# Gates of a hybrid decoder block as seven block products, their weight sums made once on GpSimd, and the router weights scaled earlier

## The chip, the cores and the metric

The kernel runs on one core of a Trainium2 chip, as one program with one launch. The metric is the device time of that core in microseconds. Three runs of the kernel before gave 1765.0, 1762.42 and 1762.63 us, median 1762.63. All arithmetic is in float32, and every float32 matmul of the program stands in the trace as two instructions.

## The reference, cut to what matters

The reference is a decoder block over 2048 tokens of 1024 channels: a normalised input goes through one wide projection, whose parts feed four mLSTM heads and a gated convolution; an output projection, a second norm, a router and 32 experts follow.

```python
hn = rms_norm(x, norm_mix)
proj = hn @ w_in + b_in                       # 1024 -> 4*512 + 2*4 + 3*512
q, k, v, o, ig, fg, cb, cc, cx = split(proj)  # o: 512 wide, ig and fg: 4 each
h_m = mlstm_chunkwise(q / sqrt(128), k, v, ig, log_sigmoid(fg))
y_m = sigmoid(o) * h_m
y_c = cb * causal_conv3(cc * cx)
x   = x + concatenate([y_m, y_c]) @ w_out
hn2 = rms_norm(x, norm_ffn)
x   = x + hier_moe(hn2, ...)                  # top-1 of 4 groups, top-2 of its 8 experts
return rms_norm(x, norm_final)
```

The change is about `o`, `ig` and `fg` (the output, input and forget gates: 520 columns of the wide projection), about the weights of the router inside `hier_moe`, and about one transpose in the expert part.

## The kernel before, in words

The tokens go through the mixer in four blocks (b = 0 to 3) of 512, 245 us each; then come the experts, from 937 us to the end. Inside a block TensorE works in this order: the q and k columns, the gates (`o` and the eight gate columns), the v columns, the convolution columns, which are woven among the mLSTM chunks (four chunks of 128 tokens), and the output projection, among whose products stand the router's logits (`router_logits`, L869) of the same block.

Nearly all of these products are block products in seven parts. A 2 x 2 split of both operands gives four block results from seven products of block sums (in place of eight products of plain blocks). `rounds` (L746) does it for q, k and the convolution, `v_part` (L808) for v, `out_part` (L775) for the output projection. The sums of weights for v and for the output projection are made once, in block 0, by GpSimd (`w_v_sums`, L1637, and `w_out_sums`, L1593), and stored to memory; later they are loaded like any weights. `weight_sums` (L1584 to L1591) makes those of the rounds anew for each slot of columns. The sums of tokens (`xsum`) are made once for each block by VectorE and serve all of them.

The gates are the exception. `tokens_out` (L779 to L789) computes them plainly: for each half s of the columns (256, and 264 with the eight gate columns in the second half) and each of four tiles of 128 tokens, eight matmuls over the 1024 input channels, into two banks of PSUM by turns; VectorE (L2368, L2370) reads each tile with its bias added and so frees its bank. In block 0 alone the gates are computed at the very start by another function.

Each engine runs its instructions in the order of the code. SyncE's queue (SP) loads the weights into two buffers `ww`, each load behind a wait for the work that frees its half; ScalarE's queue (ACT) moves keys, attention rows and `x2` rows; GpSimd's queue (POOL) has the sums, the indirect transfers and a few plain ones. At the end of a block POOL does, in this order: the `over_cleared` copy (L1708), `weight_sums(b + 1, 0)` for the first round of the next block, `norm_scales(b + 1)` (L1551, L1554), and then for each of the four tiles of the block the scale `rs2` of the second norm (L1724, L1732). For that scale ScalarE first squares the tile (`squares_of`, L1360) into the buffers `hn2`; VectorE then multiplies by it (L2274). SP brings the tile back turned by quarters into `attn` (`load_x2_quad`, L519), VectorE transposes it there (L2284), and TensorE computes the router's logits from it.

The router's weights `wrt` are multiplied once by the second norm's channel weights: eight VectorE instructions at the end of block 0 (L2575 to L2579), ahead of the reads of the output projection (`out_reads`).

In the expert part, the lists of items are built by VectorE (L2859 to L2876) while the first items already run: `hidden(1)` (L2734) and `x_turned(2)` (L2740) of item 1 and item 2 stand among the list's instructions, and TensorE's products of the next item (L1156) wait for the second.

## Time and profile before

| | |
|---|---|
| runs | 1765.0, 1762.42, 1762.63 us (median 1762.63) |
| profiled execution | 1765.43 us |
| its span, first to last instruction | 1763.7 us |
| mean granted clock of TensorE | 0.998 |
| TensorE busy | 1744.4 us, 99% of the span |
| VectorE, ScalarE, GpSimd busy | 942.2, 236.5 and 678.9 us |
| moved from and to memory | 370.78 and 68.72 MB |

The profiled execution lies 2.8 us above the median and 0.43 us above the first of the three runs. The span leaves out 1.7 us that lie around it. "Busy" counts overlapping instructions once; an engine that waits for another is not busy, and its row in a list of waits names the instruction that came last.

### The profile page before, as it was taken

The page shows a single profiled execution, that of the slowest core. Times are in us where ns is not written, and L with a number is a line of the kernel's source. Part 1 is how long each engine was busy: PE and PEld are TensorE (multiplying, and loading weights), DVE is VectorE, ACT ScalarE, POOL GpSimd, SP SyncE. Part 2 cuts the span into 40 slices and gives each one's busy share as a digit, 9 for nine tenths or more (in the row PEclk, how much of TensorE's full clock was granted, in tenths as well). Part 3 has the DMA queues.
Part 4 walks back from the last instruction along what each step waited for, and adds up shares of the span by engine and source line. Part 5 has one row for each costly group of instructions (what it writes and reads, how often), then busy time and mean ns, then how long its engine had stood idle before and what let it go on. Part 6 is the DMA issues. An engine that isn't in the chain of part 4 may idle for free. (4 is left out here: it accounts for less than half of the span.)

```text
span 1763.7 us, 27714 instructions
## 1 busy us (share of the span) xinstructions
PE 1744.4 (99%) x10013; PEld 1393.6 (79%) x10013; DVE 942.2 (53%) x1913; ACT 236.5 (13%) x618; POOL 678.9 (38%) x755
## 2 busy tenths in 40 slices
PE   9999999999999999999999999999999999999997
PEld 8889658888478887588895678887777778887776
DVE  5666785378773687763785783333423233323332
ACT  2021110211101211102210201101111101101011
POOL 4943212044221235130341125445455455554552
PEclk9999999999999999999999999999999999999999
DMA  7663742344632437423444489998988999998984
GB/s 289 229 242 109 274 168 91 123 146 170 248 117 99 144 114 272 154 95 126 155 135 140 164 329 345 349 343 326 343 349 331 339 352 338 347 341 331 349 328 174
DMA packets 135755, 415.31 MB, mean 235 GB/s; under 512 B 54838, under 2 KB 69486, under 8 KB 102320
## 3 DMA queue, kind: packets, MB, share of 16 engines
q1 hardware_dynamic: 57488, 316.78, 48.4%
q0 software_dynamic: 26880, 58.91, 9.4%
q10 hardware_dynamic: 51248, 37.82, 6.6%
q8 instruction: 81, 1.33, 0.3%
q14 instruction: 58, 0.48, 0.1%
HBM read 370.78 MB, written 68.72 MB: 249 GB/s over the span
## 5 line engine op out<-in xcount | busy, mean ns | idle before, releaser
L1134 PE MATMUL ps_proj<-hnT,wo 128*128 128x128 f32 (+4 forms) x992 | 199.5, 283 | 0.0
L1136 PE MATMUL ps_proj<-hnT,wo 128*128 128x128 f32 (+4 forms) x992 | 197.6, 281 | 0.0
L1134 PEld LDWEIGHTS ps_proj<-hnT,wo 128*128 128x128 f32 x992 | 153.7, 191 | 13.6 <-issue 13.6
L1748 POOL DMA_INDIRECT xin<-hn_rows,idx_quad x116 | 117.4, 1012 | 116.2 <-DVE hnT L2748 44.0
L1136 PEld LDWEIGHTS ps_proj<-hnT,wo 128*128 128x128 f32 x992 | 153.0, 191 | 0.0
L746 PE MATMUL ps_proj<-hnT,ww 128*128 128x256 f32 x640 | 151.9, 379 | 0.0
L746 PEld LDWEIGHTS ps_proj<-hnT,ww 128*128 128x128 f32 x640 | 119.8, 190 | 16.6 <-issue 1.4
L1584 POOL TENSOR_TENSOR xres<-ww 128x512 f32<-128x512 f32 x12 | 15.3, 1271 | 291.0 <-DMA ww<-in_w_slots 279.6
L2972 DVE SCALAR_TENSOR_TENSOR hn<-xin,rsy,ww 128x1024 f32<-128x1024 f32 x30 | 38.5, 1284 | 134.9 <-POOL rsy L1806 134.9
L1136 PE MATMUL ps_rows<-hnT,wo 128*128 128x128 f32 (+4 forms) x496 | 98.8, 281 | 0.0
L1134 PE MATMUL ps_scores<-hnT,wo 128*128 128x128 f32 (+4 forms) x496 | 98.8, 281 | 0.0
L1136 PE MATMUL ps_scores<-hnT,wo 128*128 128x128 f32 (+4 forms) x496 | 98.8, 281 | 0.0
L1134 PE MATMUL ps_rows<-hnT,wo 128*128 128x128 f32 (+4 forms) x496 | 98.8, 281 | 0.0
L775 PE MATMUL ps_proj<-wo,yT 128*128 128x512 f32 x192 | 88.8, 599 | 0.0
L787 PE MATMUL ps_proj<-ww,hnT 128*128 128x256 f32 (+1 forms) x384 | 84.7, 382 | 0.0
L2734 DVE TENSOR_TENSOR kT<-qT,ps_proj 128x128 f32<-128x128 f32 (+4 forms) x62 | 15.6, 294 | 127.4 <-ACT qT L1440 127.2
L787 PEld LDWEIGHTS ps_proj<-ww,hnT 128*128 128x128 f32 x384 | 73.0, 190 | 11.2
L1134 PEld LDWEIGHTS ps_scores<-hnT,wo 128*128 128x128 f32 x496 | 76.5, 191 | 0.0
L1136 PEld LDWEIGHTS ps_scores<-hnT,wo 128*128 128x128 f32 x496 | 76.5, 191 | 0.0
L1136 PEld LDWEIGHTS ps_rows<-hnT,wo 128*128 128x128 f32 x496 | 76.5, 191 | 0.0
L1134 PEld LDWEIGHTS ps_rows<-hnT,wo 128*128 128x128 f32 x496 | 76.5, 191 | 0.0
L746 PE MATMUL ps_proj<-xin,ww 128*128 128x256 f32 x320 | 76.4, 380 | 0.0
(522 smaller groups left out, 3494.5 us busy)
## 6 DMA issues: line engine op xcount, KB each, us to landing
wo<-in_w_gu SPq DMA_DIRECT2D x128, 1024.0 KB, 7.6
ww<-in_w_slots SPq DMA_DIRECT2D x43, 1024.0 KB, 4.9
og<-in_w_dn SPq DMA_DIRECT2D x32, 1024.0 KB
vx<-in_w_dn SPq DMA_DIRECT2D x32, 1024.0 KB
xin<-in_x SPq DMA_DIRECT2D x16, 512.0 KB, 5.8
ww<-w_v_sums SPq DMA_DIRECT2D x16, 512.0 KB, 3.9
xres<-in_x SPq DMA_DIRECT2D x16, 512.0 KB, 5.4
x_rows<-x ACTq DMA_DIRECT2D x16, 512.0 KB, 3.4
```

Of the source, the lines that this page charges most:

```text
L746: mm = pe.matmul(place, w_(k), x_[:, k, :], start=(new and k == 0), stop=(k == KH - 1), skip_group_check=True)
L775: mm = pe.matmul(place, y_[:, k, :], w_[:, k, :], start=(new and k == 0), stop=(k == KH - 1), skip_group_check=True)
L787: mm = pe.matmul(PROJ[:, n % 2, 0:w], hnT[:, k, t * P:(t + 1) * P], slot_weights(slot, k, 0, w), start=(k == 0), stop=(k == KT - 1))
L1134: pe.matmul(GU[m][:, 0:n_], wo[:, kt, m * P:(m + 1) * P], xT[:, kt, 0:n_], start=(kt == 0), stop=(kt == KT - 1), skip_group_check=True)
L1136: mm = pe.matmul(GU[m][:, CAP:CAP + n_], wo[:, kt, FF + m * P:FF + (m + 1) * P], xT[:, kt, 0:n_], start=False, stop=(kt == KT - 1), skip_g ...
L1584: pool.tensor_tensor(wsum(s, 1, first), a21, a22, ALU.add).then_inc(ready, 1)
L1748: pool.indirect_dma_start(xg[:, t * TC:(t + 1) * TC], None, hn2_d.rearrange("s (j c) -> (s j) c", j=TQ), bass.IndirectOffsetOnAxis(ap=idx_ ...
L2734: i_ = dve.tensor_tensor(hT[:, m, 0:n_], sgt[:, m, 0:n_], src[:, CAP:CAP + n_], ALU.mult)
L2972: dve.scalar_tensor_tensor(out=fo, in0=yr[:], scalar=rsy[:, 1, 0:1], in1=gfin, op0=ALU.mult, op1=ALU.mult).then_inc(S_("out_rows_ready"), 1)
```

## The change

It has four parts.

1. In blocks 1 to 3 `o_part` (L842 after) computes the gates as seven products of eight matmuls with 260 columns each: a weight slot now holds 256 columns of `o` and four gate columns in each half. The seven products go into four pairs of banks (`NUM`, `SR`, `STA`, `PROJ`), eight VectorE instructions (`o_reads`) put the results together, and SP loads their weights half a slot at a time (`load_o`).
2. The four sums of gate weights are made in block 0 by GpSimd and stored as `wg_d` (`load_w_gates`, `w_gate_sums`). The columns are cut in two: the first 128 columns of every input block with the four gate columns (j = 0), and the other 128 (j = 1). The buffers are `attn`, the tail slots and `hn2`; the instructions stand on GpSimd between the `over_cleared` copy of block 0 and the scales of the second norm. ScalarE's `squares_of` of tiles 0 and 1 and SP's `load_x2_quad` wait for the last store (`SUMS_STORED`).
3. The eight scalings of `wrt` move from the end of block 0 to its v products: three ahead of the first read of v, five behind it.
4. `x_turned(2)` moves ahead of seven small instructions of the item list, right behind `hidden(1)`.

```diff
-    WG = WC + 2 * H
+    WG = WC + H
-            def tokens_out(b, kind, s, t, slot, first):
-                n = number[(kind, (s, t))]
...
-                w = WG if slot == OG else WC
-                for k in range(KT):
-                    mm = pe.matmul(PROJ[:, n % 2, 0:w], hnT[:, k, t * P:(t + 1) * P], slot_weights(slot, k, 0, w),
-                                   start=(k == 0), stop=(k == KT - 1))
+            def o_part(b, i):
+                s, n = o_loaded(b, i)
+                pe.wait_ge(s, n)
...
+                if i in (2, 3, 4):
+                    pe.wait_ge(S_("o_read"), o_read(b, {2: "p1", 3: "u2", 4: "c22"}[i]))
+                x_ = {1: hnT[:, 0:KH, 0:TH], 2: hnT[:, KH:KT, 0:TH], 3: hnT[:, KH:KT, TH:TB],
+                      4: xsum[3], 5: xsum[0], 6: xsum[1], 7: xsum[2]}[i]
+                w_ = o_place(i).rearrange("p (k c) -> p k c", c=WG)
+                for m in range(2):
+                    for k in range(KH):
+                        mm = pe.matmul(O_BANK[i][:, m, 0:WG], x_[:, k, m * P:(m + 1) * P], w_[:, k, :],
+                                       start=(i not in (2, 4) and k == 0), stop=(k == KH - 1), skip_group_check=True)
+                mm.then_inc(S_("o_part_done"), 1)
...
-                for s in range(2 if b > 0 else 0):
-                    for t in range(CT):
-                        tokens_out(b, "o", s, t, 4 + s, t == 0)
+                for i, buf, half in (V_PARTS if b > 0 else ()):
+                    o_part(b, i)
...
                 def squares_of(t):
+                    if t < 2:
+                        act.wait_ge(S_("w_v_sums_stored"), SUMS_STORED)
...
+            def load_w_gates(j):
+                if j == 0:
+                    pool.wait_ge(S_("update_done"), CT)
+                else:
+                    pool.wait_ge(S_("part_done"), part_end(0, NS - 1, 4))
+                for n in range(4):
+                    for at, tiles in gate_sums_views(j):
+                        src = w_slots[4 + n // 2, :, (n % 2) * OQ:(n % 2 + 1) * OQ].rearrange("p (k c) -> p k c", c=WG)
+                        pool.dma_start(tiles[n], src[:, :, at]).then_inc(S_("w_v_loaded"), 16)
+            def w_gate_sums(j):
...
+                pool.wait_ge(S_("w_v_loaded"), 64 + (128 if j == 0 else 192))
+                for step, (to, first, op, second) in enumerate(((3, 2, ALU.add, 3), (2, 0, ALU.subtract, 2),
+                                                                (0, 3, ALU.subtract, 0), (1, 1, ALU.subtract, 0))):
+                    for at, tiles in views:
+                        i_ = pool.tensor_tensor(tiles[to], tiles[first], tiles[second], op)
+                    i_.then_inc(made, 1)
+                    pool.wait_ge(made, 4 + j * 4 + step + 1)
+                for n, a in enumerate((3, 0, 2, 1)):
+                    for at, tiles in views:
+                        dst = wg_d[n].rearrange("p (k c) -> p k c", c=WG)[:, :, at]
+                        pool.dma_start(dst, tiles[a]).then_inc(S_("w_v_sums_stored"), 16)
...
+                with pool.If(b < 1):
+                    load_w_gates(0)
+                    w_gate_sums(0)
+                    load_w_gates(1)
                 with pool.If(b < NB - 1):
                     weight_sums(b + 1, 0)
...
                 with pool.If(b < NB - 1):
                     norm_scales(b + 1)
+                with pool.If(b < 1):
+                    w_gate_sums(1)
...
+                router_weights(range(3))
                 v_reads(("p1",))
+                router_weights(range(3, KT))
...
-                dve.wait_ge(S_("consts_loaded"), 16 * NCONST)
-                if b < 1:
-                    for k in range(KT):
-                        i_ = dve.tensor_scalar(wrt[:, k, :], wrt[:, k, :], gffn_c[:, k:k + 1], None, ALU.mult)
-                    i_.then_inc(S_("router_consts"), 1)
...
                     if n_ == NE:
                         hidden(1)
+                        x_turned(2)
...
-                    if n_ == NE:
-                        x_turned(2)
```

On GpSimd at the end of block 0 the kernel before has, from the `over_cleared` copy to the first scale of the second norm (`og` holds the sums of the next block's first round, `ssx` and `st` the scales):

```order
L1708 DMA hn_rows<-in_x 16x16384
L1584 TENSOR_TENSOR og<-ww 128x512 [waits yn_ready]
L1587 TENSOR_TENSOR og<-og,ww 128x512 [waits wsum_ready]
L1588 TENSOR_TENSOR og<-ww 128x512
L1591 TENSOR_TENSOR og<-ww,og 128x512 [waits wsum_ready]
L1551 TENSOR_SCALAR ssx<-ssx 128x4 [waits ss_ready]
L1554 TENSOR_TENSOR ssx<-ssx,mhalf 128x4 [waits ms_ready]
L1724 TENSOR_SCALAR st<-st 128x1 [waits ss2_ready]
L1732 TENSOR_TENSOR st<-st,mhalf 128x1 [waits hn2_ready,ms2_ready]
```

The changed kernel has at the same place (one of each repeated pair of loads, sums and stores is shown, the last column of a DMA is its pieces):

```order
L1802 DMA hn_rows<-in_x 16x16384
L1731 DMA attn<-in_w_slots 128x4x128 [waits update_done]
L1731 DMA slots_tail<-in_w_slots 128x4x4
L1741 TENSOR_TENSOR attn<-attn 128x512 [waits w_v_loaded]
L1747 DMA w_gate_sums<-attn 512x1x128 [waits w_v_sums_made]
L1747 DMA w_gate_sums<-slots_tail 512x1x4
L1731 DMA hn<-in_w_slots 128x4x128 [waits part_done]
L1642 TENSOR_TENSOR og<-ww 128x512 [waits yn_ready]
L1609 TENSOR_SCALAR ssx<-ssx 128x4 [waits ss_ready]
L1741 TENSOR_TENSOR hn<-hn 128x512 [waits w_v_loaded]
L1747 DMA w_gate_sums<-hn 512x1x128 [waits w_v_sums_made]
L1824 TENSOR_SCALAR st<-st 128x1 [waits ss2_ready]
```

Between the copy and the first scale now stand 12 loads, 12 instructions of sums and 12 stores; the sums of the next block's first round are behind 20 of these DMAs, and the first scale of the second norm is behind all of them.

On TensorE the gates of a later block stand in the kernel before, between the k columns (L746) and the v columns, as eight tiles, of which these are the first, the second, the third and the fifth:

```order
L787 MATMUL ps_proj<-ww,hnT 128x256 [waits sums_out,w_loaded0]
L787 MATMUL ps_proj<-ww,hnT 128x256 x7
L787 MATMUL ps_proj<-ww,hnT 128x256 [waits sums_out]
L787 MATMUL ps_proj<-ww,hnT 128x256 [waits bank_emptied]
L787 MATMUL ps_proj<-ww,hnT 128x264 [waits bank_emptied,w_loaded1]
```

In the changed kernel they are these products, each with seven more matmuls behind the one that carries the waits:

```order
L842 MATMUL ps_num<-ww,hnT 128x260 [waits yn_ready,w_loaded0]
L842 MATMUL ps_scores_rows<-ww,xin 128x260 [waits out_read,slots_ready,second_loaded0]
L842 MATMUL ps_state<-ww,xin 128x260 [waits logits_emptied,out_read,w_loaded1]
L842 MATMUL ps_num<-ww,hnT 128x260 [waits o_read,second_loaded1]
L842 MATMUL ps_proj<-ww,xin 128x260 [waits sums_out,w_loaded0]
L842 MATMUL ps_state<-ww,hnT 128x260 [waits o_read,w_loaded1]
L842 MATMUL ps_scores_rows<-ww,xin 128x260 [waits o_read,second_loaded1]
```

Eight tiles became seven products of the same number of matmuls, over six banks more, and each product now waits for its own half slot of weights.

## Rows read from the trace of the kernel before

**Rows 1.** The page, part 1: busy us, share of the span, instructions.

```profile
PE 1744.4 (99%) x10013; PEld 1393.6 (79%) x10013; DVE 942.2 (53%) x1913; ACT 236.5 (13%) x618; POOL 678.9 (38%) x755
```

**Rows 2.** Timeline, TensorE and VectorE, block 1 (start, us, engine, line, form).

```profile
304.49 28.22 PE L787 MATMUL ps_proj<-ww,hnT 128*128 128x256 f32 x128
332.54 3.62 PE L808 MATMUL ps_proj<-ww,hnT 128*128 128x256 f32 x16
...
305.95 0.17 DVE L2167 SCALAR_TENSOR_TENSOR slot_i<-rank,expert 128x8 int32<-128x8 f32 x1
```

**Rows 3.** DMA issues of the whole span: size each, median us to landing.

```profile
ww<-in_w_slots SPq DMA_DIRECT2D x14, 512.0 KB, 4.1
```

**Rows 4.** Timeline, VectorE and TensorE, block 0's end and v columns.

```profile
200.75 4.48 DVE L2578 TENSOR_SCALAR wrt<-wrt,by_channel 128x64 f32<-128x64 f32 x8
206.99 0.69 DVE L2465 TENSOR_TENSOR uu<-uu,yT 128x512 f32<-128x512 f32 x1
...
207.78 3.67 PE L775 MATMUL ps_proj<-kT,uu 128*128 128x512 f32 x8 [2.20 <-issue]
...
86.06 4.82 DVE L2362 TENSOR_TENSOR bvd<-bias 128x256 f32<-128x256 f32 x1
90.91 0.69 DVE L2343 TENSOR_TENSOR vx<-ps_proj,bias 128x512 f32<-128x512 f32 x1
...
96.30 1.89 PE L808 MATMUL ps_proj<-ww,hnT 128*128 128x256 f32 x8
```

**Rows 5.** Timeline, VectorE and TensorE, the item lists of the expert part.

```profile
1051.33 0.28 DVE L2734 TENSOR_TENSOR kT<-qT,ps_rows 128x128 f32<-128x128 f32 x1
...
1055.34 0.63 DVE L2740 STREAM_TRANSPOSE hnT<-xin 128x256 f32<-128x256 f32 x1 [0.18 <-DVE idx_out L2874]
...
1056.03 1.98 PE L1156 MATMUL ps_num<-og,kT 128*128 128x512 f32 x4 [1.05 <-DVE hnT L2740]
```

**Rows 6.** Timeline, TensorE, GpSimd and VectorE, the end of block 0.

```profile
185.57 1.06 PE L992 MATMUL ps_state<-vx,attn 128*128 128x129 f32 x8
...
201.16 1.28 POOL L1584 TENSOR_TENSOR og<-ww 128x512 f32<-128x512 f32 x1 [18.28 <-DMA ww<-in_w_slots]
...
209.75 1.37 POOL L1554 TENSOR_TENSOR ssx<-ssx,mhalf 128x4 f32<-128x4 f32 x1
...
228.01 0.19 POOL L1724 TENSOR_SCALAR st<-st 128x1 f32<-128x1 f32 x1 [2.60 <-ACT hn L1360]
...
220.56 0.87 DVE L1963 TENSOR_SCALAR zz<-ident,ssx 128x128 f32<-128x128 f32 x4
```

**Rows 7.** GpSimd's groups of DMA issues: busy us, mean ns, idle before.

```profile
L1748 POOL DMA_INDIRECT xin<-hn_rows,idx_quad x116 | 117.4, 1012 | 116.2 <-DVE hnT L2748 44.0 <-DVE hnT L2740 42.9 <-issue 26.5
...
L1603 POOL DMA_DIRECT2D w_out_sums<-x x2 | 1.1, 556 | 0.0
...
L1671 POOL DMA_DIRECT2D slots<-slots_main x1 | 0.5, 521 | 0.0
```

**Rows 8.** DMA issues: of 187 to 199 us, then a store of the whole span.

```profile
ww<-in_w_slots SPq DMA_DIRECT2D x1, 1024.0 KB, 13.6
...
w_v_sums<-xres POOLq DMA_DIRECT2D x2, 512.0 KB, 4.0
```

**Rows 9.** Timeline, ScalarE, SyncE's queue, VectorE, TensorE: block 0's first tiles.

```profile
226.67 1.06 ACT L1360 ACTIVATE hn<-x 128x1024 f32<-128x1024 f32 x1 [2.28 <-DVE x L2632]
...
225.94 7.11 SPq L519 DMA_DIRECT2D attn<-x_rows  x8
...
228.88 1.29 DVE L2274 SCALAR_TENSOR_TENSOR hn<-x,st,late 128x1024 f32<-128x1024 f32 x1 [1.77 <-POOL st L1732]
...
233.36 2.10 DVE L2284 STREAM_TRANSPOSE hn2T<-attn 128x512 f32<-128x512 f32 x2
...
236.27 1.09 PE L869 MATMUL ps_state<-hn2T,wrt 128*64 128x128 f32 x16
```

**Rows 10.** Timeline, TensorE at the start of the span.

```profile
1.24 4.87 PE L849 MATMUL ps_rows<-ones 128*128 128x128 f32 x24 [1.24 <-POOL ones L1495]
```

More of the change, by code:

```diff
@@ L152, in build @@
         x2 = [x2_pair[:, i, :] for i in range(2)]
-        hn2 = [sb(f"hn2_{i}", [P, D]) for i in range(2)]
+        hn2_pair = sb("hn2", [P, 2, D])
+        hn2 = [hn2_pair[:, i, :] for i in range(2)]
         rows = [buf[0:H, j * TB:(j + 1) * TB] for buf in (*x2, *hn2) for j in range(2)]
@@ L593, in _ @@
+                for used, i in ((1, 5), (6, 3), (2, 4)):
+                    sp.wait_ge(S_("v_part_done"), v_part_end(b, used))
+                    own_instruction(sp)
+                    load_v(b, i)
+                for n in range(8, SLOTS_B):
                     slot_free(sp, b, n - 2)
@@ L1279, in _ @@
                     own_instruction(act)
-                exp_o(0)
-                exp_o(1)
+                for n, (s, t) in enumerate(EXP_ORDER):
+                    if n % 2 == 0:
+                        act.wait_ge(S_("o_read"), o_read(b, ("c11", "c22", "d12", "c21")[n // 2]))
+                    half = og4[:, t, s, 0:WC]
+                    act.activation(half, half, ACT.Exp, scale=-1.0).then_inc(S_("exp_o_ready"), 1)
+                    act.wait_ge(S_("exp_o_ready"), 2 * (b * 2 * CT + n) + 1)
+                    own_instruction(act)
+                    act.activation(half, half, ACT.Copy, bias=1.0).then_inc(S_("exp_o_ready"), 1)
                 with act.If(b < 1):
@@ L3051, in _packed @@
         cols += [conv + dm + s * wc, conv + 2 * dm + s * wc, conv + s * wc]
-    w_slots = np.zeros((len(cols), P, d // P * (wc + h2)), np.float32)
+    hh = h2 // 2
+    w_slots = np.zeros((len(cols), P, d // P * (wc + hh)), np.float32)
     for n, c in enumerate(cols):
-        w = by_partition(w_in[:, c:c + wc + (h2 if c + wc == gates else 0)])
+        more = gates + (n - 4) * hh if n in (4, 5) else 0
+        w = by_partition(np.concatenate([w_in[:, c:c + wc], w_in[:, more:more + (hh if more else 0)]], axis=1))
         w_slots[n, :, :w.shape[1]] = w
```

259 lines of the change are left out of this document (164 added, 95 removed).

## The prediction

> **What bounds the kernel now.** I read the totals of the engines first. TensorE is busy for 1744.4 us, 99% of the span [rows 1], so the time changes only by fewer or shorter TensorE instructions, by an end of one of TensorE's waits, or by a new wait. Then I read TensorE's rows, where the time between two starts is the price, then the rows of the engines that feed it at the four places of the change, and last the prices of GpSimd's DMA issues and the times to their landing.
>
> **The gates (part 1).** In block 1 the gates begin at 304.49 and the v columns at 332.54: 28.05 us for eight tiles, 128 instructions [rows 2]. Half of them have 256 columns and half 264, so 0.2191 us is the price of one with 260, and that is what all of the new ones have. Seven products of 16 instructions take 112 x 0.2191 = 24.5 us, 3.5 less. With three blocks that is **-10.5 us**.
>
> Does anything eat it? The products need half slots of 512 KB, which land 4.1 us after their issue [rows 3], and SP can issue each of them some 7 us, two products, ahead. The v columns of the kernel before are loaded half by half as well, and the row of TensorE's that begins with the first of them shows no wait [rows 2]. The second product also waits for the routing slots of the block before, which VectorE makes at 305.95 [rows 2]; it would start at 308.0. So I take nothing. The reads take a bank pair each: a VectorE read of 512 columns of PSUM costs 0.69 [rows 4], eight of them 5.6 of 24.5 us. The weight sums for the gates are 260 wide in place of 256, nothing beside it. In block 0 the first gates have 260 columns in both halves (64 instructions of 256 and 64 of 264 before): no difference.
>
> **The router's weights (part 3).** Before, eight scalings hold VectorE from 200.75 for 4.48 us; the sums of tokens behind them end at 207.68, and TensorE's next product starts at 207.78 after 2.20 us of waiting [rows 4]. Without the scalings that wait ends (4.48 earlier is more than 2.20), at this place **-2.2 us**. It counts only if nothing later in block 0 waits anyway, see below. At their new place, 86 to 96 us, VectorE is at the biases for 4.82 us and reads the first v product at 90.91, and TensorE's third v product needs that read at 96.30 [rows 4]. Ahead of the read now come a second such instruction and three scalings (0.56 each at the old price, 1.7). If the second one isn't held, 0.7 like the read, they fit into the 5.4 us that are free, with 0.69 for the read; if it takes 4.82 like the first, TensorE waits 1.8. I take nothing, and 1.8 as the upper end.
>
> **The transpose (part 4).** TensorE waits 1.05 us for the transpose at 1055.34, and `hidden(1)` ends at 1051.6, so it can stand 3.7 us earlier [rows 5]. **-1.0 us**; behind it the hidden products feed on, and the lists of items, 0.6 us later, aren't waited for.
>
> **GpSimd's sums (part 2).** This is what the prediction turns on. The trace has no such DMA, so I follow the queue from the last step of block 0's cell state, 186.6 [rows 6].
> - Eight loads. A POOL issue of 128 rows costs 0.556, of 32 rows 0.521 [rows 7], which is 0.36 ns a row; with 512 pieces I get 0.70. The lower bound is 0.556 (rows cost nothing more), the upper the 1.01 of an indirect issue with the 0.23 of idle time that stands before each (26.5 of "issue" for 116) [rows 7], 1.24. I take 0.70, the nearest. The loads are issued by 192.2. Between 187 and 199 a load of SP took 13.6 us to its landing [rows 8], so the DMA engines are far from idle, and I let the last piece land 6 us after its issue, at 198.2 (the lower end is 194.5, the upper 216 to 221, if the small pieces get through only behind SP's loads).
> - Sums of j = 0: four steps one behind the other, each 1.28 and a small one of 0.19 and a wait of about 0.18 [rows 6], and 1 us for VectorE's instructions that share the port with them: 7.6, until 205.8.
> - Eight stores and four loads, 12 x 0.70 = 8.4 and 0.3: 214.5.
> - The sums of the next block's first round start at 201.16 before and take 5.2 (four of 1.28 and a wait); they end now at 219.7. Then the scales of the next block, 1.7: 221.4. Before, they ended at 211.1, and VectorE first used them at 220.56 [rows 6]; the 0.9 us by which it is late there only hold up work that waits longer further on.
> - Sums of j = 1: 4 x (1.28 + 0.18) = 5.8, and four stores, the last issued at about 229.8; a store of such a size landed 4.0 after its issue [rows 8]. **The last store is there at 233.8.**
>
> Who waits? ScalarE's squares of tiles 0 and 1 and SP's loads into `attn`. The square of tile 1 starts at 226.67 before, and SP's load at 225.94 [rows 9]. The squares come in a row on ScalarE, so that of tile 1 starts 1.7 us after the release, at 235.5: 8.8 later. From there it goes by the order before: the scale on GpSimd at 228.01 [rows 6], VectorE's multiplication at 228.88, the transpose of the tile out of `attn` at 233.36, done 2.10 later, and the router's logits on TensorE at 236.27 [rows 9], with 0.8 us to spare. SP's loads go 7.9 later and come to the same. All else in VectorE's queue behind the multiplication, the output products' reads too, is late by the same. So the logits start **8.0 us** later than before.
>
> That takes the gain of part 3: the earlier 2.2 us of TensorE only make it wait longer at the logits. Its worth is nothing. It waits for some 8 to 10 us there, over four times its wait at 207.78. What follows a rest is seen at the start of the span: 24 filler matmuls of 128 columns take 4.87 us there [rows 10], and eight of 129 columns 1.06 in the middle of the block [rows 6], from start to start about 0.11, so 24 would be 2.8; the start from rest cost 2 us. I take **+2.0** for the clock, which would be at its lower level, 1.2 GHz, for a while after such an idle stretch (bounds 0 and 4).
>
> **Sum**, against the profiled execution's 1765.43 (span 1763.7 and 1.7 around it): -10.5 - 1.0 + 8.0 + 2.0 = -1.5, 1763.9. The profiled execution lies 2.8 above the median of the runs, so I put the new median at 1762.63 - 1.5 = 1761.1 and up, **1762**, within 0.2% (3.5 us) of it, which is what a measurement of this kernel can tell from no change.
>
> **A rule of the Trainium skill.** GpSimd's issue price has the largest lever: of the chain to the last store some 15 issues lie in it, after the loads of j = 0, so 0.1 us more costs 1.5. The Trainium skill, "DMA: Bandwidth & Descriptors", section "Anatomy of one DMA — SWDGE (gpsimd) path", says that many descriptors can be written before their cost shows. By that 512 pieces cost what 128 do, 0.556, and the time is that of A below. In the other direction goes "SBUF — State Buffer", section "SBUF: two separate sides": GpSimd can't write descriptors while VectorE holds the port pair that they share. VectorE's 4.82 us for a sum of 256 columns beside GpSimd's sums [rows 4] agrees with the lock, in the other sense. No run here shows it for descriptors.
>
> **Rivals.**
> - *A, quicker queue.* Each issue costs 0.556 and the loads land at their lower end, 194.5. The stores are then 3.7 + 15 x 0.14 = 5.8 earlier in place, at 228, and the logits are late by 8.0 - 5.8 = 2.2 to 4; with 1 to 2 for the clock: -11.5 + 3 + 1.5 = -7, **1756**. For it: the flat issue prices of 32 and 128 rows [rows 7]. Against: SP's slow load at the same time [rows 8]. It would be fully hidden, at -13.7, **1749**, if the last store landed by 223, for which the chain would have to be 11 us shorter than mine; A's 5.8 is all that the rows give.
> - *B, slower: dear pieces.* If a DMA of 512 pieces is paid like an indirect one, 1.24, the chain grows by 15 x 0.54 = 8.1 us, and all of it reaches the logits: -1.5 + 8.1 = +6.6, **1769 to 1771**. It decides from 0.80 us for one issue (there the sum is nought; at 1.03 it is +3.5). For it: the indirect issues, 116 of one line alone, are the only ones in the trace that cost more than 0.7, and no row shows a direct one of 512 pieces, so the step from 0.556 may be a large one. If besides the small pieces wait behind SP's loads (13.6 us to their landing [rows 8]), the loads of j = 0 land at 216 to 221 and the logits are late by 26 to 31 us: **1782**.
> - *C, the gates don't come cheaper*: 512-KB loads, drains or banks hold TensorE between the products (each would have to lose 0.5 us a product to undo it). For it: 16 waits stand ahead of the seven products; against: the v columns without a wait [rows 2]. With the stall it would be 1772.
> - *D, the clock stays up*: 2 less, **1760**. For it: the 2.20 us of idle time at 207.78, after which the products keep their 3.6 us [rows 4]; against: these are a quarter of what is to come.
>
> **How the numbers follow.** My sum with D, 1759 to 1765: 0.42. A: 0.24 (fully hidden 0.04 of it). B: 0.22 (0.07 of it the second part). C: 0.07. A remainder of 0.05 lies on both sides. The range 1755 to 1776 holds my sum, most of A and the first part of B and C; outside are full hiding and SP's loads ahead, some 0.15 to 0.2. Faster by over 0.2% is below 1759.1: A, and the lower edge of my sum with D, 0.34. Slower is above 1766.2: B, C and a part of the remainder, 0.34. Between them 0.32.
>
> **What would show it.** Right, if the v columns of block 1 start 24.5 us after the gates; if GpSimd's issues with 512 pieces last 0.6 to 0.8 us; if ScalarE's square of tile 0 ends an idle stretch at 234 with the store as its releaser; if the logits of tile 0 follow an idle TensorE of 8 to 10 us near 244; if the waits at 207.78 and 1056.03 are gone. Wrong, if TensorE has no idle time at the end of block 0, or one of over 14 us, or if the gaps between the gates' products exceed those inside them.

## The result, and the profile after

The changed kernel takes 1775.79 us (median of 4 runs, 1773.32 to 1777.41) against 1762.53 of the kernel before on the same chip (4 runs): ratio 1.0064 [1.005, 1.0079], slower by 13 us. Each experiment below is compared in the same way with the kernel before on its own chip, where that kernel's median was 1762.5 to 1764.4. The profiled execution of the changed kernel took 1775.77, with a span of 1774.0; that is 10.3 more than the 1763.7 of before, whose profiled execution lay 2.9 above its median.

TensorE does less, as planned. Part 1 of the page of the changed kernel answers to [rows 1]:

```profile
PE 1738.3 (98%) x9965; PEld 1386.4 (78%) x9965; DVE 945.5 (53%) x1898; ACT 234.7 (13%) x618; POOL 708.9 (40%) x791
```

48 instructions (16 in each of three blocks) and 6.1 us of busy time are gone, and the span has grown by 10.3: 16.4 us are new idle time. The list of TensorE's waits in the changed kernel (source line, releaser, us in total, times, longest) shows where it lies (a releaser "issue" means that the profile shows nothing that the engine waited for):

```profile
PE ps_state L927 <- issue: 11.5, 1, 11.5
PE ps_scores_rows L872 <- DVE zz L2063: 5.2, 1, 5.2
PE ps_state L1216 <- issue: 1.9, 1, 1.9
...
PE ps_scores_rows L1177 <- DVE hnT L2858: 1.2, 1, 1.2
```

The 2.20 at 207.78 [rows 4] and the 1.05 at 1056.03 [rows 5] are gone, and two smaller ones have come up in the experts (1.9 and 1.2, the last two lines). TensorE's timeline in the changed kernel (start, us, engine, line, form, and in brackets the idle time before it with its releaser) shows the end of block 0 and the gates of block 1:

```profile
205.33 3.60 PE L817 MATMUL ps_proj<-kT,uu 128*128 128x512 f32 x8
...
219.06 3.60 PE L817 MATMUL ps_scores_rows<-vx,yT 128*128 128x512 f32 x8
227.91 2.05 PE L872 MATMUL ps_scores_rows<-zz,ones 128*128 128x512 f32 x2 [5.25 <-DVE zz L2063]
229.75 5.44 PE L817 MATMUL ps_proj<-wo,yT 128*128 128x512 f32 x8
...
238.46 3.60 PE L817 MATMUL ps_proj<-kT,cc 128*128 128x512 f32 x8
253.56 1.98 PE L927 MATMUL ps_state<-hn2T,wrt 128*64 128x128 f32 x16 [11.51 <-issue]
...
260.14 3.60 PE L817 MATMUL ps_scores_rows<-qT,cc 128*128 128x512 f32 x8
...
323.57 3.67 PE L842 MATMUL ps_num<-ww,hnT 128*128 128x260 f32 x16
...
348.11 3.62 PE L865 MATMUL ps_proj<-ww,hnT 128*128 128x256 f32 x16
```

The seven gate products go from 323.57 to 348.11 in steps of 3.50 or 3.51 without a gap: 24.54 us for the 28.05 of [rows 2]. The loss lies ahead of them. The norm rows (L872) wait 5.25 us, the router's logits of tile 0 (L927) 11.51, and the logits start at 253.56 instead of 236.27 [rows 9], 17.3 late. What the logits wait for is VectorE's transpose of the tile, which ends at 253.45. The products behind either wait take longer than their 3.60. The windows of the changed kernel (stretch, its length, busy us of PE, PEld, DVE, ACT and POOL with counts, then the granted clock, DMA share, GB/s) say why:

```profile
228.00:230.00 2.00, 2.00 (x3) 0.97 (x4) 1.90 (x4) 0.00 (x0) 0.00 (x0) 0.50 0.93 320
...
253.00:257.00 4.00, 3.44 (x18) 2.44 (x19) 3.66 (x6) 0.28 (x1) 0.00 (x0) 0.50 0.00 0
257.00:263.00 6.00, 6.00 (x16) 2.70 (x15) 5.28 (x7) 0.00 (x0) 0.00 (x0) 0.97 0.00 0
```

Behind each wait the granted clock is 0.50, the level of 1.2 GHz, and 0.97 to 1.00 a few microseconds later. GpSimd's timeline in the changed kernel shows the chain that the logits wait for, at the place of [rows 6]:

```profile
186.84 0.80 POOL L1731 DMA_DIRECT2D attn<-in_w_slots  x1 [4.01 <-PE ps_state L1052]
...
192.07 0.75 POOL L1731 DMA_DIRECT2D slots_tail<-in_w_slots  x1
205.09 1.26 POOL L1741 TENSOR_TENSOR attn<-attn 128x512 f32<-128x512 f32 x1 [12.27 <-DMA slots_tail<-in_w_slots]
...
211.41 0.72 POOL L1747 DMA_DIRECT2D w_gate_sums<-attn  x1 [0.29 <-POOL slots_tail L1741]
...
216.51 3.77 POOL L1731 DMA_DIRECT2D hn<-in_w_slots  x4
219.53 2.04 POOL L1642 TENSOR_TENSOR og<-ww 128x512 f32<-128x512 f32 x1
...
225.81 1.04 POOL L1612 TENSOR_TENSOR ssx<-ssx,mhalf 128x4 f32<-128x4 f32 x1
230.56 5.29 POOL L1741 TENSOR_TENSOR hn<-hn 128x512 f32<-128x512 f32 x4 [3.71 <-DMA hn<-in_w_slots]
236.15 3.00 POOL L1747 DMA_DIRECT2D w_gate_sums<-hn  x4 [0.29 <-POOL hn L1741]
```

In this chain GpSimd stands still twice, for its own loads: 12.27 us for those of j = 0 and 3.71 for those of j = 1. The last store lets ScalarE go at 242.72 (timeline of ScalarE, changed kernel: the square of tile 0; that of tile 1 follows at 243.78, where [rows 9] has 226.67):

```profile
242.72 1.06 ACT L1418 ACTIVATE hn<-x 128x1024 f32<-128x1024 f32 x1 [29.11 <-DMA w_gate_sums<-hn]
```

The DMA issues of two stretches of the changed kernel, 187 to 207 and 206 to 245 us (form, queue, count, KB each, median us to landing), answer to [rows 8]:

```profile
ww<-in_w_slots SPq DMA_DIRECT2D x2, 1024.0 KB, 21.2
attn<-in_w_slots POOLq DMA_DIRECT2D x4, 256.0 KB, 8.7
...
hn<-in_w_slots POOLq DMA_DIRECT2D x4, 256.0 KB, 11.2
```

GpSimd's loads took 9 to 11 us each. SP's two slot loads took 21.2 on the median; the one issued at 187.17, which is that of [rows 8], took 19.3 instead of 13.6. From 190 to 205 the windows show a DMA share of 0.96 to 1.07: the 16 DMA engines were full. In the kernel before they were full as well from 190 to 199 (0.97 to 1.05). Two windows of the changed kernel, columns as above:

```profile
193.00:196.00 3.00, 3.00 (x16) 2.64 (x15) 1.84 (x4) 0.00 (x0) 0.00 (x0) 1.00 1.06 377
221.00:224.00 3.00, 1.66 (x4) 0.38 (x2) 0.00 (x0) 0.00 (x0) 2.82 (x3) 1.00 1.01 121
```

In the second, while the loads of j = 1 are under way, the engines are as full, but they move a third of the bytes (e9 returns to it).

### The profile page after: what moved, and what is told of

It reads as the page before. It is cut to its first block and busy times, and to the rows that moved or that the text cites. A ratio compares the mean times of both kernels' runs of the same rounds, so it can differ in the third digit from the quotient of the medians.

```text
span 1774.0 us, 27704 instructions
## 1 busy us (share of the span) xinstructions
PE 1738.3 (98%) x9965; PEld 1386.4 (78%) x9965; DVE 945.5 (53%) x1898; ACT 234.7 (13%) x618; POOL 708.9 (40%) x791
## 3 DMA queue, kind: packets, MB, share of 16 engines
q0 software_dynamic: 28416, 63.17, 10.3%
## 5 line engine op out<-in xcount | busy, mean ns | idle before, releaser
L1196 PE MATMUL ps_scores_rows<-hnT,wo 128*128 128x128 f32 (+4 forms) x992 | 197.7, 281 | 0.0
L1194 PE MATMUL ps_scores_rows<-hnT,wo 128*128 128x128 f32 (+4 forms) x992 | 197.7, 281 | 0.0
L1194 PEld LDWEIGHTS ps_proj<-hnT,wo 128*128 128x128 f32 x992 | 153.8, 191 | 13.6 <-issue 13.6
L1194 PEld LDWEIGHTS ps_scores_rows<-hnT,wo 128*128 128x128 f32 x992 | 153.0, 191 | 0.0
L1196 PEld LDWEIGHTS ps_scores_rows<-hnT,wo 128*128 128x128 f32 x992 | 153.0, 191 | 0.0
L788 PE MATMUL ps_proj<-xin,yT 128*128 128x256 f32 x312 | 72.3, 381 | 0.4 <-POOL yT L1645 0.4
L3053 DVE SCALAR_TENSOR_TENSOR xin<-ps_state,wgt,xin 128x512 f32<-128x512 f32 x31 | 23.3, 751 | 91.2 <-DMA xin<-x_rows,idx 90.6
L817 PEld LDWEIGHTS ps_proj<-wo,yT 128*128 128x128 f32 x192 | 36.4, 196 | 40.1 <-issue 39.4
L788 PEld LDWEIGHTS ps_proj<-xin,ww 128*128 128x128 f32 x320 | 60.6, 190 | 8.6 <-issue 0.5
L788 PE MATMUL ps_proj<-xin,xres 128*128 128x256 f32 x288 | 66.1, 379 | 0.0
L788 PEld LDWEIGHTS ps_proj<-xin,yT 128*128 128x128 f32 x312 | 58.5, 190 | 8.8 <-issue 1.3
```

Source lines behind the costliest of these rows:

```text
L788: mm = pe.matmul(place, w_(k), x_[:, k, :], start=(new and k == 0), stop=(k == KH - 1), skip_group_check=True)
L817: mm = pe.matmul(place, y_[:, k, :], w_[:, k, :], start=(new and k == 0), stop=(k == KH - 1), skip_group_check=True)
L1194: pe.matmul(GU[m][:, 0:n_], wo[:, kt, m * P:(m + 1) * P], xT[:, kt, 0:n_], start=(kt == 0), stop=(kt == KT - 1), skip_group_check=True)
L1196: mm = pe.matmul(GU[m][:, CAP:CAP + n_], wo[:, kt, FF + m * P:FF + (m + 1) * P], xT[:, kt, 0:n_], start=False, stop=(kt == KT - 1), skip_g ...
L3053: dve.scalar_tensor_tensor(out=h_, in0=y, scalar=wgt[:, col:col + 1], in1=h_, op0=ALU.mult, op1=ALU.add).then_inc(S_("y_emptied"), 1)
```

## The experiments

**e1: the change without the sums.** The seven products read plain halves of the weights, and nothing is loaded, added or stored on GpSimd for them. The gates are then other numbers and so is the routing; only the stages up to the output projection of block 3 compare. Its time, 2311 us, has other work of the experts in it and says nothing here.

```diff
-                with pool.If(b < 1):
-                    load_w_gates(0)
-                    w_gate_sums(0)
-                    load_w_gates(1)
...
-                with pool.If(b < 1):
-                    w_gate_sums(1)
```

> The changed kernel without the sums of gate weights: GpSimd makes none, nobody waits for their stores, and the four products that need sums load plain halves of the gate weights in their place, so the gates of blocks 1 to 3 are other numbers. Theory: all that the change loses is lost at the end of block 0, in TensorE's waits of 5.25 and 11.51 us and the low clock behind each. Then what is left is the gain of the gates (3 x 3.5), of the router's weights (2.2) and of the transpose (1.05), less the 3.1 us of new waits that the changed kernel has in the expert part: 1762.5 - 10.5 - 2.2 - 1.05 + 3.1 = 1752, and 1749 if those waits aren't of the change. No idle time of TensorE above 1 us between 198 and 300 us. Rival: the seven products or their reads and loads cost something too, in blocks 1 to 3; then the time is above 1757 and the gates' stage takes more than 24.6 us.

TensorE's timeline at the start of that projection, in the kernel before, the changed kernel and e1:

```profile
935.87 3.60 PE L775 MATMUL ps_proj<-wo,yT 128*128 128x512 f32 x8
...
945.02 3.60 PE L817 MATMUL ps_proj<-wo,yT 128*128 128x512 f32 x8
...
922.19 3.60 PE L817 MATMUL ps_proj<-wo,yT 128*128 128x512 f32 x8
```

(The experts' products follow from 1004 us in the kernel before, and not from 937, as its description in words has it.) So the seven products and the moved scaling bring 13.7 by themselves, and the sums at the end of block 0 cost 22.8. In e1 TensorE has no wait over 0.5 us between 62 and 989, and the seven products take the same 24.54 us. The loss up to the experts is in this one place; no product, drain or bank takes any (rival C falls).

**e2 and e3: one small part alone, in the kernel before.** e2 moves only the transpose, e3 only the router's scalings.

```diff
                         hidden(1)
+                        x_turned(2)
...
-                    if n_ == NE:
-                        x_turned(2)
```

> The kernel before with the transpose of item 2 right behind the hidden products of item 1, nothing else. Theory 1 (the prediction's): TensorE's wait of 1.05 us near 1056 goes, nothing comes in its place: 1761.5. Theory 2 (from the trace of the changed kernel): with that wait gone, the weights of the next item are loaded a microsecond earlier, while the rows of x gathered for item 0 are still under way; these land some 6 us later, VectorE adds them late, and TensorE waits 1.9 us at the next item: 1763.4, no gain or a small loss.

> The kernel before with the router's weights scaled among the value products, nothing else. Theory: the wait of 2.20 us at 207.78 goes and no other one comes in block 0, since the stall at the logits that ate it in the changed kernel is not there: 1760.3. Rival: some other wait of block 0's end takes its place (the logits stand 0.8 us behind VectorE's transposes): 1762 to 1762.5.

e2: 1763.01 against 1763.57, ratio 0.9988 [0.9979, 0.9997]; the wait of 1.05 is gone and none comes in its place. e3: 1762.3, ratio 0.9992 [0.9983, 1.0001]; the wait of 2.20 is gone and the gates of block 1 start at 301.38 in place of 304.49. In the traces each does what the prediction priced, and both intervals hold that price; e3's also holds no change, so its time alone would not show the gain.

**e4 and e5: the sums at the start of block 0**, from weights that lie in the buffers `ww` for TensorE anyway: ScalarE copies two halves, GpSimd adds into `x2`, `attn` and `slots_tail`, which are free there. e4 stores them through SP's queue, e5 through ScalarE's.

```diff
             load_w_v()
+            gate_sum(0)
+            gate_sum(1)
+            gate_sum(2)
             weight_sums(0, 0)
+            gate_sum(3)
...
+                            for m, a in enumerate((2, 0, 3, 1)):
+                                for c in range(2):
+                                    at = (slice(0, WC), slice(WC, WG))[c]
+                                    sp.dma_start(wg_d[m].rearrange("p (k c) -> p k c", c=WG)[:, :, at], gate_places(a)[c]
```

> The changed kernel with the same sums made elsewhere: at the start of block 0, from the gate weights that lie in the weight buffers for the first gates anyway (no loads). ScalarE copies the first slot's two halves into x2, GpSimd makes three sums from 20 us on and the fourth behind the sums of the first round, SyncE's queue stores them behind the router's weights. Nothing of the gates is left at the end of block 0. Theory: the stall at the end of block 0 was a matter of the place only; here GpSimd is idle from 22 to 29 and from 37 to 41 us, and the four sums take 10.5 us, so nearly nothing waits: 1750 to 1753. Rival 1: the sums push GpSimd's sums of the first round (29.0 us, needed at 37.6) behind, TensorE waits 2 to 6 us near 38: 1753 to 1758. Rival 2: eight stores among the loads of 36 to 52 us hold up the weights of the second slot: a wait near 48, the same price.

> The kernel with the sums at the start of block 0 again, with one difference: the eight stores of the sums go through ScalarE's queue, behind its exponentials (47 us), in place of SyncE's. In the run before this, TensorE waited 10.63 us at 71.65 for the weights of the fourth slot, whose load stood in SyncE's queue behind these stores (issued from 41.4 to 62.1, where the load was issued at 48.15 without them), and 1.32 at 117. Theory: that queue was all of it; without it the time is 1765.8 - 12 = 1754, or below, with no idle time of TensorE over 1 us before 900 us. Rival: the stores' small pieces hold up the DMA engines themselves, whichever queue they come from; then the fourth slot's weights or those of the value products are late by 3 us or more again: above 1757.

e4: 1765.83 against 1763.57, ratio 1.0007 [0.9998, 1.0016]. The waits at the end of block 0 are gone, but there is a new one; the timeline of TensorE and of SP's queue (e4):

```profile
71.65 3.67 PE L809 MATMUL ps_proj<-hnT,ww 128*128 128x256 f32 x8 [10.63 <-DMA ww<-in_w_slots]
...
42.75 7.04 SPq L611 DMA_DIRECT2D w_gate_sums<-x  x1
49.84 4.19 SPq L611 DMA_DIRECT2D w_gate_sums<-slots_tail  x1
...
62.13 1.36 SPq L551 DMA_DIRECT2D ww<-in_w_slots  x2
```

The eight stores hold SP from 41.40 to 62.09, two of them for 7.04 and 4.19 us, and the next weights, issued at 48.15 in the changed kernel, go out at 62.13. My expectation of 1750 to 1753 left that out; my second rival named it, at 2 to 6 us. e5: 1760.22 against 1764.0, ratio 0.9981 [0.9972, 0.999]; I expected 1754. The blocked issues now stand on ScalarE, where they hold up no load of weights, but the stores land late, and GpSimd, which waits for them ahead of the output weights' sums, makes TensorE wait 6.08 us at 81.41. Timelines of ScalarE's queue and of GpSimd (e5):

```profile
49.53 8.25 ACTq L1367 DMA_DIRECT2D w_gate_sums<-slots_tail  x1
...
73.67 4.93 POOL L1698 TENSOR_TENSOR hn<-wo 128x512 f32<-128x512 f32 x4 [8.37 <-DMA w_gate_sums<-slots_tail]
```

**e6: another order on GpSimd at the old place**: all loads first, then every sum, the scales of the next block among them, all stores last.

```diff
                     load_w_gates(0)
-                    w_gate_sums(0)
                     load_w_gates(1)
+                    w_gate_sums(0)
...
                     w_gate_sums(1)
+                    store_gate_sums(0)
+                    store_gate_sums(1)
```

> The changed kernel with the same work on GpSimd at the end of block 0 in another order: both groups of loads first, then the sums of j = 0, the sums of the next block's first round and the scales of its norm, the sums of j = 1, and all twelve stores last. Theory: the first idle stretch (5.25 us, for the scales) goes, since the scales end near 218 and are needed near 219; the second stays in good part, since the stores are still issued one by one and land at 235 to 240, against 242 before: 1760 to 1766. Rival: the DMA engines are the limit and not the order, the loads only land later when they are issued together; then the stall at the logits is as long or longer, and the sum stays at 1772 to 1778.

1773.03 against 1764.0, ratio 1.0049 [1.0034, 1.0064]; I expected 1760 to 1766. Timelines of GpSimd, TensorE and ScalarE (e6):

```profile
204.63 1.26 POOL L1744 TENSOR_TENSOR attn<-attn 128x512 f32<-128x512 f32 x1 [2.49 <-DMA slots_tail<-in_w_slots]
...
234.36 3.60 PE L817 MATMUL ps_proj<-kT,cc 128*128 128x512 f32 x8
251.32 1.98 PE L927 MATMUL ps_state<-hn2T,wrt 128*64 128x128 f32 x16 [13.36 <-issue]
...
240.48 1.06 ACT L1418 ACTIVATE hn<-x 128x1024 f32<-128x1024 f32 x1 [23.16 <-DMA w_gate_sums<-hn]
```

The loads of j = 0 land as late as in the changed kernel. The norm rows no longer wait (they start at 226.64; a wait of 3.62 at 219.67 has come up ahead of them), and TensorE begins its last product ahead of the logits at 234.36, 4.1 earlier than in the changed kernel. Yet the logits start only 2.24 earlier, and that is just what the last store gains (240.48 for 242.72), since the stores now come behind everything. So the logits go by the last store, and the first wait is contained in the second.

**e7 and e11: the clock.** Idle matmuls ahead of the two waits keep TensorE busy, so that the cost of the low clock can be told from that of the wait; they fill the waits and don't shorten them. In e7 there are 23 and 50 matmuls (two instructions each), in e11 23 and 63.

```diff
+            def keep_warm(n):
+                for i in range(n):
+                    pe.matmul(NUM[:, 1, 0:P], ident[:], ident[:], start=True, stop=True)
...
+                if b == 1:
+                    keep_warm(23)
...
+                if isinstance(g, int) and g == 0:
+                    keep_warm(50)
```

> The changed kernel with idle matmuls on TensorE ahead of the two waits at the end of block 0 (23 of 128 columns ahead of the norm's rows, 50 ahead of the first logits), whose results nobody reads. They fill the waits of 5.25 and 11.51 us and no more. Theory: the low clock behind each wait costs 2.8 and 1.8 us; with it gone the products behind the waits take 3.44 us from start to start again, and the time is 4.6 less: 1771. Rival: the products are slow there for another reason (the DMA traffic, or late operands); then they stay slow and the time is 1775 to 1777.

> The changed kernel with idle matmuls ahead of both waits at the end of block 0 again, 63 in place of 50 ahead of the first logits; with 50, TensorE still stood idle for 3.06 us there and the products behind were slow again (2.08 for two instructions that take 1.12). Theory: with the wait filled to under 0.5 us the products behind the logits take 3.44 us from start to start and the clock costs nothing: 1.6 to 1.8 us less than with 50. Rival: what makes them slow is not TensorE's rest; then they stay slow.

e7: 1774.06 against 1764.0, ratio 1.0058 [1.0042, 1.0073], between my 1771 and the rival's 1775 to 1777. The products behind the first wait are back at 3.43 from start to start, and the logits start at 253.16, as late as without (253.56): the low clock behind the first wait is contained in the second wait. The fillers end 3.06 us short of the logits, and the products behind are slow again (granted clock 0.65 from 253 to 257). e11, a single run, took 1771.03; TensorE's timeline (e11):

```profile
254.71 1.09 PE L935 MATMUL ps_state<-hn2T,wrt 128*64 128x128 f32 x16
...
259.49 3.60 PE L817 MATMUL ps_scores_rows<-qT,cc 128*128 128x512 f32 x8
```

With the clock at 1.00 throughout, the logits and the products up to that at 259.49 take 4.78 us; in the changed kernel the same stretch, 253.56 to 260.14, takes 6.58. The clock costs 1.8 us, once. The total of e11 is 4.8 below that of the changed kernel; what the other 3 are is open, and a single run on another chip doesn't tell.

**e8 and e12: SP's loads out of the way of GpSimd's.** e8 holds back SP's loads of tokens and all behind them until the loads of j = 0 have landed, e12 also the two before them (`vx` and a slot, 2 MB). The edit of e12 is shown; that of e8 has the same three lines behind these two loads.

```diff
                 own_instruction(sp)
+                with sp.If(b < 1):
+                    sp.wait_ge(S_("w_v_loaded"), 64 + 128)
+                    own_instruction(sp)
                 sp.dma_start(vflat[:, 0:KH * 512], wt_d[2]).then_inc(S_("w_out_sum_loaded4"), 16)
```

> The changed kernel in which SyncE's queue issues the loads of block 1's tokens and of the second slot (7 transfers, 5 MB) only after GpSimd's eight gate loads of j = 0 have landed. Theory: these were late (205.0 in place of 198) because they shared the DMA engines with SyncE's loads; apart, they land by 197 to 200, the sums of j = 0 start 5 to 8 us earlier, while SyncE's loads end 3 to 6 us later; the stall at the logits gets shorter by 2 to 6 us unless the tokens' loads become what is late: 1770 to 1774. Rival: the 512-piece loads are slow by themselves; then they land at 203 to 205 again, SyncE's loads are late by 10 us, and the time is 1780 or more.

> The changed kernel in which all of SyncE's loads at the end of block 0 wait until GpSimd's gate loads of j = 0 have landed: those of the third output sum and of the next block's first slot too (2 MB, issued at 187 before), which the run with the tokens' loads held back had left in front. In that run, and in the one with whole rows, the gate loads landed at 206.5 and 205.0 as before. Theory: they wait behind and beside these two loads on full DMA engines; with both held back only 3 MB issued at 182 to 184 are in front, the gate loads land by 194 to 199, and the last store comes 5 to 9 us earlier than at 242.7; the time falls to 1767 to 1772 if the held loads don't become late themselves. Rival: the software queue's loads are slow whatever else is under way; then they land at 203 or later, all of SyncE's loads are late by 16 us, and the time is 1782 or more.

e8: 1774.93, ratio 1.0055 [1.004, 1.0071]; j = 0 landed at 206.48, 13.03 us after the last issue, so not sooner. e12: 1772.36 against 1764.15, ratio 1.0044 [1.0027, 1.006]. GpSimd's timeline (e12):

```profile
200.84 1.39 POOL L1744 TENSOR_TENSOR attn<-attn 128x512 f32<-128x512 f32 x1 [7.44 <-DMA slots_tail<-in_w_slots]
...
229.95 5.29 POOL L1744 TENSOR_TENSOR hn<-hn 128x512 f32<-128x512 f32 x4 [4.64 <-DMA hn<-in_w_slots]
```

The loads of j = 0 land 4.2 earlier (205.09 to 200.84), 7.44 us after their last issue in place of 12.27. The engines are no longer full for all of that time: their share is 1.06 from 193 to 196, 0.79 from 196 to 199 and 0.38 from 199 to 202. But the sums meet VectorE now and take longer (1.70 in place of 1.26 for some), the loads of j = 1 come in as late as ever, and at 229.95 only 0.6 of the 4.2 is left (230.56 in the changed kernel).

**e9: the same bytes in 128 pieces** of whole rows of the weights (2048 and 32 bytes) in place of 512 (512 and 16).

```diff
-                        src = w_slots[4 + n // 2, :, (n % 2) * OQ:(n % 2 + 1) * OQ].rearrange("p (k c) -> p k c", c=WG)
-                        pool.dma_start(tiles[n], src[:, :, at]).then_inc(S_("w_v_loaded"), 16)
+                        src = w_slots[4 + n // 2, :, (n % 2) * OQ:(n % 2 + 1) * OQ]
+                        pool.dma_start(tiles[n], src[:, at]).then_inc(S_("w_v_loaded"), 16)
```

> The changed kernel with the gate weights cut in two along whole rows in place of along columns, at the same place and in the same order: each of GpSimd's loads and stores has 128 pieces of 2048 B (and of 32 B for the rest of a row) where it had 512 of 512 B (and of 16 B). The bytes and the sums are the same, the DMAs are 32 in place of 24, the pieces 4096 in place of 12288. Theory: the small pieces made the loads and stores slow. Then an issue costs 0.56 again, the loads of j = 0 land by 198 to 201 (205.0 in the changed kernel), the last store by 226 to 232 (242), and the time falls by 10 to 16 us to 1760 to 1766, still with a stall at the logits, since the squares want the buffers at 221. Rival: the DMA engines are full with bytes from 187 to 217, whatever the pieces; then the loads land at 204 to 206 again and the time is 1772 to 1777.

1770.94 against 1764.38, ratio 1.0032 [1.002, 1.0044], where I expected 1760 to 1766. GpSimd's timeline, a window and the DMA issues of 215 to 220 us (e9):

```profile
187.74 0.54 POOL L1728 DMA_DIRECT2D slots_tail<-in_w_slots  x1
...
204.98 1.25 POOL L1738 TENSOR_TENSOR attn<-attn 128x512 f32<-128x512 f32 x1 [13.46 <-DMA slots_tail<-in_w_slots]
...
226.34 1.26 POOL L1738 TENSOR_TENSOR hn<-hn 128x512 f32<-128x512 f32 x1
...
221.00:224.00 3.00, 1.99 (x5) 0.57 (x3) 0.00 (x0) 0.00 (x0) 2.82 (x4) 1.00 1.03 378
...
hn<-in_w_slots POOLq DMA_DIRECT2D x4, 256.0 KB, 5.7
```

An issue costs 0.54. j = 0 lands at 204.98, where it landed with 512 pieces: their number is not what makes these loads late. For j = 1 the pieces, of these loads or of the stores ahead of them, do matter: with 128 the loads land in 5.7 us in place of 11.2, the wait of 3.71 for them is gone, and the full DMA engines move 378 GB/s from 221 to 224 in place of 121.

**e10: early sums with whole-row stores.** e5 with stores of 128 rows of 4096 (and 64) bytes, and with the wait for them moved to the second step of the output weights' sums, where a buffer of theirs is first needed. These are two edits to e5; their shares were not told apart.

```diff
-                            act.dma_start(wg_d[m].rearrange("p (k c) -> p k c", c=WG)[:, :, at], gate_places(a)[c]
+                            act.dma_start(wg_d[m, :, at], gate_places(a)[c]
...
-                    own_instruction(pool)
-                    pool.wait_ge(S_("consts_loaded"), 16 * NCONST)
                     for k in range(KH):
...
+                pool.wait_ge(S_("consts_loaded"), 16 * NCONST)
```

> The kernel with the sums at the start of block 0, stored through ScalarE's queue, with two differences from the run of that kind before: each sum is cut into 1024 and 16 columns of a whole row (128 pieces of 4096 B and of 64 B) in place of 256 and 4 of each input channel block (512 pieces), and the wait for the stores stands ahead of the second part of the output projection's sums, which overwrites x2, in place of the first. In the run before, GpSimd waited 8.37 us for the stores (issued from 47.4 to 68.3) ahead of those sums, and TensorE 6.08 at 81.41 behind it. Theory: the stores are issued within 5 us and landed by 60, nothing waits for them, and the time is 1760.2 less 6 to 7: 1752 to 1754.5. Rival: 2 MB more on the DMA engines between 47 and 62 us hold up the third and fourth slots' weights (a wait of TensorE at 60 to 65): 1755 to 1758.

**1755.42 us** (median of 5, 1753.32 to 1756.38) against 1764.38 of before, ratio 0.9942 [0.9928, 0.9955]: faster than both kernels, and a little above the 1752 to 1754.5 that I expected. ScalarE's queue and TensorE's timeline (e10):

```profile
47.72 0.33 ACTq L1367 DMA_DIRECT2D w_gate_sums<-attn  x1
...
51.81 0.58 ACTq L1367 DMA_DIRECT2D w_gate_sums<-slots_tail  x1
...
235.97 1.09 PE L941 MATMUL ps_state<-hn2T,wrt 128*64 128x128 f32 x16
```

The eight stores are issued in 4.7 us (20.9 in e5), and the end of block 0 runs in step, the logits at 235.97 without a wait. Of the 13.7 that e1 shows up to the output projection of block 3, 10.0 are there (925.87 for 935.87), and 9.0 in the medians; short waits near 44, 64 and 105 us (0.84, 0.71, 0.79) take part of the rest.

## Why the prediction was wrong

I forecast no change, 1762, and it came out 13 us slower. The time lies just inside my range, among the cases that I gave to rival B, but by luck: B's mechanism (1.24 us for an issue) isn't what happened. An issue of 512 pieces cost 0.75, close to my 0.70 and below the 0.80 from which B was to decide. It wasn't A's flat price either (128 pieces cost 0.54 in e9). Nearest to what happened is B's second part, loads that land late; I had them at 216 to 221 and only together with dear issues (and its 1782 leaves out the 8.1 us of these issues), where they came at 205.09.

- *Gates, -10.5*: right but for 0.6. 24.54 us for seven products, predicted 24.5, no gaps; from the gates of block 1 to the projection of block 3 the changed kernel gains 9.9 (the delay goes from 19.1 to 9.15), e1 11.0.
- *Router, -2.2, eaten by the stall*: right. The wait is gone, e3's trace shows its worth alone, and the second biases instruction on VectorE took 1.38 without holding anyone.
- *Transpose, -1.0*: right by itself (e2). In the changed kernel 1.3 is gained there, and two new waits of 1.23 at 1031.32 and 1.90 at 1085.03 give back more. For the second the trace shows a path: the gather of rows for the next tile went out at 1068.46 and VectorE got its rows at 1078.71, while SP's 4 MB of expert weights started 3.7 us behind it; before it is 1058.12, 1062.56 and 5.5 us. These waits differ from variant to variant, and what sets them stays open.
- ***The last store is there at 233.8*: this step failed.** It was there at 242.7. Of the 8.9, 6.9 are the landing of j = 0 (205.09; I let the last piece land 6 us after its issue, it took 12.3), and 3.7 the wait for the loads of j = 1, which I had at nothing without a reason; in e9, with 128 pieces in the loads and in the stores ahead of them, it is gone. The other steps together were some 1.7 shorter than I had them: sums of j = 0 6.0 for 7.6, stores and loads 8.4 for 8.7, the sums of the next block's first round 6.0 for 5.2, scales 1.4 for 1.7, sums of j = 1 5.3 for 5.8, stores 3.3 for 2.6, the last landing 3.6 for 4.0.
- *The way from the store to the logits, 10.5*: 10.9. So the logits were late by 17.3, not 8.0: the 8.9 and this 0.4.
- *The scales' 0.9, harmless*: wrong in size and in kind, right in the total. With the chain late they came at 226.85, not 221.4, and TensorE stood 5.25 us for the norm rows. But e6 shows that the logits don't come sooner without this wait: they follow the last store.
- *The clock, +2.0*: right, 1.8 by the stretch in e11.

With the measured terms the sum closes on the profiled executions: 17.3 + 1.8 - 9.9 = 9.2 at the output projection of block 3 (9.15), and at the end, with the experts' -1.3 and the two new waits, it gives 11.0 where 10.3 was measured; the 0.7 between is not explained.

Why were the loads of j = 0 late? I had set 6 us between the 4.0 of a store and the 13.6 of SP's load [rows 8]; the 13.6 was the row of the same stretch, the nearest, and I went by less than half of it, though the engines were full in the kernel before, too (0.97 to 1.05 from 190 to 199). What the runs show: it is not their pieces (e9) and not SP's later loads (e8); SP's 2 MB ahead account for 4.8 of the 12.3 us (e12). Why 1 MB through GpSimd's queue needs the other 7.4 stays open. They also show that no repair at this place wins the loss back: against the kernel before on the same chip e6, e8, e9 and e12 are 9.0, 10.9, 6.6 and 8.2 us slower, the changed kernel 13.3. In e6 and e12 a gain at one link of the chain met the next link that was late. The rival I gave 0.04, full hiding, is had only by moving the sums elsewhere (e10).

## What to carry to other kernels

When an edit hangs a chain of load, sum and store into a stretch, take the landing times from a transfer of the same stretch and see its DMA share first; here the engines were full, and another order of the links (e6) gained the logits 2.2 of 17.3 us. Put work that is done once where its engine and its buffers are idle and its inputs already on the chip (e10), and move data in whole rows (e9, e10). Where several waits follow one another on the bounding engine, only the one set by the longest chain counts: in e6 the norm rows waited no more and TensorE was 4.1 us sooner at the logits, but these moved by the last store's 2.24.

## What was not expected of the hardware

- The number of pieces of a store weighs on the engine whose queue issues it: stores of 512 pieces held SP or ScalarE for up to 7.04 and 8.25 us in one issue (e4, e5), those of 128 for 0.33 to 0.85 (e10). On GpSimd 512 pieces cost 0.75 and 128 pieces 0.54 an issue (e9).
- DMA engines that are full need not move much: a share of 1.01 went with 121 GB/s from 221 to 224 in the changed kernel, and one of 1.03 with 378 in e9, where the same bytes go in a third of the pieces.
- The clock doesn't follow from the length of the idle time alone: it fell behind 3.06 (e7) and 3.34 us (e12, the norm rows at 226.37), and not behind 3.62 (e6, at 219.67, where the next product came after 3.54). TensorE had been busy without a gap ahead of each, with filler matmuls in e7 and with products of the output projection in e6 and e12. The windows of e6 and of e12 behind those waits (columns as above):

```profile
219.60:222.00 2.40, 2.33 (x6) 1.14 (x7) 2.06 (x5) 0.00 (x0) 2.24 (x3) 1.00 0.82 338
```

```profile
228.00:230.00 2.00, 2.00 (x3) 0.68 (x2) 1.51 (x3) 0.00 (x0) 0.05 (x1) 0.50 1.03 407
```

  The granted clock is 1.00 in e6, the full level of 2.4 GHz, and 0.50 in e12, that of 1.2. Why, no run here shows.
- A sum of 128x512 on GpSimd takes 1.26 us with VectorE idle (changed kernel, 205 to 211) and up to 1.70 beside VectorE's work, one of 128x16 0.22 and up to 0.67 (e8, e12).
